# The first norm's sums of squares: six tiles added up on GpSimd, two TensorE matmuls behind the first linear tile in place of eight among the transposes

## The reference

```
def rms_norm(x, g):
    y = x * lax.rsqrt(jnp.mean(x * x, axis=-1, keepdims=True) + EPS)
    return y * g
...
h = rms_norm(x, attn_norm[0])
q, k, v = jnp.split(h @ w_in[0], 3, axis=-1)      # then stick-breaking attention
```

## Time and profile before

| | us |
|---|---|
| median of three runs | 2217.3 (2216.12 to 2218.74) |
| the profiled execution | 2217.15 |
| its span | 2215.4 |
| TensorE busy | 2183.6 (99%) |
| VectorE busy | 1376.4 (62%) |
| ScalarE busy | 794.3 (36%) |
| GpSimd busy | 0.2 |

### The profile page before, as it was taken

One profiled execution on the slowest core, in us unless ns is written; L12 is line 12 of the kernel. 1 busy time (PEld: TensorE's weight loads), 2 busy tenths in 40 slices (PEclk: granted clock), 3 DMA queues, 4 the chain that ended last, 5 costly groups with the idle time before them and its releaser, 6 DMA issues.

```text
span 2215.4 us, 28343 instructions
## 1 busy us (share of the span) xinstructions
PE 2183.6 (99%) x10140; PEld 1728.5 (78%) x10140; DVE 1376.4 (62%) x2081; ACT 794.3 (36%) x1161; POOL 0.2 (0%) x4
## 2 busy tenths in 40 slices
PE   8999999999999999999999999999999999999998
PEld 6777788888886666788888877787788878888887
DVE  6666655554448887755554476687855557888733
ACT  5555432222225555322222224457632223222222
POOL 0000000000000000000000000000000000000000
PEclk9999999999999999999999999999999999999999
DMA  4112133333332222233333332222233332333332
GB/s 143 57 57 57 48 100 99 95 95 92 103 90 58 62 62 58 86 95 97 100 95 97 92 81 67 58 67 67 62 105 95 95 99 87 100 98 95 95 101 91
DMA packets 367107, 188.31 MB, mean 85 GB/s; under 512 B 8968, under 2 KB 366265, under 8 KB 367033
## 3 DMA queue, kind: packets, MB, share of 16 engines
q1 hardware_dynamic: 367033, 187.30, 29.6%
HBM read 185.18 MB, written 2.10 MB: 85 GB/s over the span
## 4 chain that ended last, share of the span: by engine, by line
PE 89%; DVE 6%; ACT 2%; issue 2%; DMA 0%; DVEq 0%; SPq 0%; ACTq 0%
PE lin L1742 78%; PE S L1805 1%; PE ob L1836 1%; PE S L1818 1%; PE S L1915 1%; DVE conv L1381 1%; PE ob L1944 1%; ACT w_hi L534 1%; PE lin L1770 1%; PE misc L1928 1%; PE S L1823 1%; ACT L805 0%; PE S L2071 0%; DVE w_lo L931 0%; PE ob L2099 0%
## 5 line engine op out<-in xcount | busy, mean ns | idle before, releaser
L534 ACT ACTIVATE w_hi<-raw 128x1024 fp32r<-128x1024 f32 x361 | 381.5, 1057 | 844.8 <-PE lin L1742 815.4
L931 DVE TENSOR_TENSOR w_lo<-raw,w_hi 128x1024 fp32r<-128x1024 f32 x361 | 440.9, 1222 | 207.2 <-ACT w_hi L534 206.3
L1742 PE MATMUL lin<-h_hi,w_hi 128*128 128x512 f32 x1928 | 496.1, 399 | 0.6
L1742 PE MATMUL lin<-h_lo,w_hi 128*128 128x512 f32 x1928 | 482.1, 392 | 0.0
L1742 PE MATMUL lin<-h_hi,w_lo 128*128 128x512 f32 x1928 | 477.9, 390 | 0.0
L1742 PEld LDWEIGHTS lin<-h_hi,w_hi 128*128 128x128 f32 x1928 | 358.8, 188 | 89.9 <-issue 15.9
L1742 PEld LDWEIGHTS lin<-h_hi,w_lo 128*128 128x128 f32 x1928 | 361.0, 188 | 74.3
L1742 PEld LDWEIGHTS lin<-h_lo,w_hi 128*128 128x128 f32 x1928 | 358.9, 188 | 74.5 <-issue 1.0
L1742 PE MATMUL lin<-gu_hi,w_hi 128*128 128x512 f32 x528 | 131.4, 389 | 0.0
L1742 PE MATMUL lin<-gu_hi,w_lo 128*128 128x512 f32 x528 | 131.4, 389 | 0.0
L1742 PE MATMUL lin<-gu_lo,w_hi 128*128 128x512 f32 x528 | 131.4, 389 | 0.0
(11 more groups left out here) (380 smaller groups left out, 2172.2 us busy)
## 6 DMA issues: line engine op xcount, KB each, us to landing
raw<-in_w_in_dram SPq DMA_DIRECT2D x108, 512.0 KB, 3.7
raw<-in_w_gate_dram SPq DMA_DIRECT2D x44, 512.0 KB, 3.7
raw<-in_w_up_dram SPq DMA_DIRECT2D x44, 512.0 KB, 3.7
raw<-in_ffn_up_dram SPq DMA_DIRECT2D x44, 512.0 KB, 3.7
raw<-in_w_down_dram SPq DMA_DIRECT2D x32, 512.0 KB, 3.7
raw<-in_w_out_dram SPq DMA_DIRECT2D x24, 512.0 KB, 3.7
raw<-in_ffn_down_dram SPq DMA_DIRECT2D x16, 512.0 KB, 3.7
raw<-in_w_down_dram SPq DMA_DIRECT2D x16, 384.0 KB, 3.4
```

The costliest lines, as they stand in the source:

```text
L534: act.activation(w_hi[u.slot][:, :, :], raw[u.slot][:, :, :], ACT.Copy).then_inc(hi_ready, 1)
L931: dve.tensor_tensor(w_lo[u.slot][:, :, :], raw[u.slot][:, :, :], w_hi[u.slot][:, :, :].bitcast(f32), ALU.subtract).then_inc(lo_ready, 1)
L1742: ins = pe.matmul(acc, (wh, wh, wl)[part][:, k, :], (hi, lo, hi)[part][:, k0 + k, :], start=first and part == 0 and k == 0, stop=last and ...
```

## The change

GpSimd gets six additions. The first adds the squares of tiles 0 and 1 into `xt[0]`, the next five add tiles 2 to 6. Each waits for ScalarE's square (`sq_ready`) and for the addition before it (`x_acc`). Tile 7's square stays in `sq_sum`. TensorE's eight `x_squares` matmuls go; two take their place behind the whole first linear tile, one over `xt[0]` and one over `sq_sum`. ScalarE's square of tile f now waits until GpSimd has read the buffer it overwrites (`x_acc`), and the scale waits for the one `x_sq`.

```
-        x_sq = sem("x_sq")
+        x_sq, x_acc = sem("x_sq"), sem("x_acc")
...
                 if f >= 2:
-                    act.wait_ge(x_sq, f - 1)
+                    act.wait_ge(x_acc, max(f - 2, 1))
...
-            act.wait_ge(x_sq, KT)
+            act.wait_ge(x_sq, 1)
             token_scale(0)
...
+        @block.gpsimd
+        def _(pool):
+            pool.wait_ge(sq_ready, 2 + CREDIT)
+            pool.tensor_tensor(xt[0][:, :], sq[:, :], sq_sum[:, :], ALU.add).then_inc(x_acc, 1)
+            for f in range(2, KT - 1):
+                pool.wait_ge(sq_ready, f + 1 + CREDIT)
+                pool.wait_ge(x_acc, f - 1)
+                pool.tensor_tensor(xt[0][:, :], xt[0][:, :], (sq, sq_sum)[f % 2][:, :], ALU.add).then_inc(x_acc, 1)
...
                 first_rows(range(KT - 2))
-                x_squares(KT - 2)
                 first_rows([KT - 2])
-                x_squares(KT - 1)
                 first_rows([KT - 1])
                 pe.wait_ge(resid, 3 * (R_INIT + 7))
                 linear(At(0), 0, (1, 2), late=late)
+                x_squares()
                 linear(At(0), 1, (0,))
...
-            def x_squares(f):
-                pe.wait_ge(sq_ready, f + 1 + CREDIT)
-                pe.matmul(misc[:, :], table("ones"), (sq, sq_sum)[f % 2][:, :], start=f == 0, stop=f == KT - 1).then_inc(x_sq, 1)
+            def x_squares():
+                pe.wait_ge(x_acc, KT - 2)
+                pe.wait_ge(sq_ready, KT + CREDIT)
+                pe.matmul(misc[:, :], table("ones"), xt[0][:, :], start=True, stop=False)
+                pe.matmul(misc[:, :], table("ones"), sq_sum[:, :], start=False, stop=True).then_inc(x_sq, 1)
...
                 ins.then_inc(x_tr, 1)
-                if f > 1:
-                    x_squares(f - 2)
```

## The result

The changed kernel takes 2222.12 us (median of 18 runs, 2220.19 to 2222.87), the kernel before 2217.15 (18 runs, 2216.02 to 2218.78): ratio 1.0021, 95% interval 1.0014 to 1.0027. It is slower by 5 us. That lies in the range (2216.6 to 2222.4) near its upper end, with five of the 18 runs above it, and beyond the forecast of 2219.6. The profiled execution took 2221.91, its span 2220.1.

A forecast was written before the change was run, and what follows sets the result against it. TensorE was taken as the bound, with the first linear tile's eighth row waiting on weight DMA, ScalarE and VectorE. Net 0.79 (1.72 - 0.93) plus 1.7 for the clock gave 2.5 us on 2217.15: 2219.6, range 2216.6 to 2222.4.

The forecast's parts named there:

- a fall of the clock without turns: Main case: TensorE at 1.2 GHz when the first linear tile starts, GpSimd and VectorE not excluding each other; 2219.6 us, chance 0.38.
- turns and a drop: Rival: `h_lo` and GpSimd's additions exclude each other, and TensorE's clock falls; 2221.0 us, chance 0.24.
- The two squares behind the tile: Two square matmuls behind the first linear tile, where TensorE has no gap, cost 2 x 0.86 = 1.72 us.
- The eighth row's gain: First linear tile's eighth row, freed from the last two square matmuls, ends at 20.98 instead of 21.91: 0.93 us gained.
- What goes ... they return nothing: Six square matmuls before 18.34 return nothing when removed; what follows is bound by weight DMA, ScalarE and VectorE.
- The addition's duration: Each GpSimd addition taken as 1.22 us, bounded by 0.69 and 2.44, from VectorE rows.
- the 1.7 us from which ScalarE's later squares would have waited: Addition length at which GpSimd's fifth sum would be late for ScalarE's square 7 at 19.20, without turns.
- Turns on the port: Rival: VectorE's `h_lo` and GpSimd's additions exclude each other, making `h_hi` 7 1.4 us late; 0.24 with a clock drop.
- The clock: Thin TensorE stretch before the eighth row drops it to 1.2 GHz at the first linear tile, for 3.40 us: 1.7 us.
- The bound of 2.3: Upper bound in us on the cost of TensorE's clock drop at the first linear tile; lower bound 0.
- The late scale, ScalarE's queue: `rsB` by about 28.0, still in time; first softplus 0.3 us later than TensorE's shift, covered by 2.3; cost 0.
- a slow GpSimd: Rival: GpSimd becomes the bound; at 1.8 us an addition with turns, 6.8 us in all, 2223.9; chance 0.11.

The follow-up runs named there:

- e7: Changed kernel plus six idle-time TensorE matmuls, behind the transposes of tiles 6 and 7 and before rows 5 to 7 of the first linear tile; 2220.4 us, ratio 1.0010.
- e8: Changed kernel with six idle-time TensorE matmuls added and GpSimd's additions removed (squares of tiles 0 to 5 left out of the sum); 2218.5 us, ratio 1.0006.
- e4: Kernel before without its first six square matmuls and ScalarE's waits for them, the last two in place, nothing on GpSimd; 2220.0 us, ratio 1.0003.
- e6: Kernel before, reordered only: transposes of tiles 6 and 7 and four first-linear-tile rows issued ahead of tile 4's square; 2217.0 us, ratio 0.9996.
- e2: Changed kernel without GpSimd's additions and ScalarE's waits for them (squares of tiles 0 to 5 left out of the sum); 2221.4 us, ratio 1.0013.
- e9: Changed kernel with GpSimd's six additions reading `xT`, ScalarE's waits removed, squares of tiles 0 to 5 left out of the sum; 2222.5 us, ratio 1.0016.
- e1: Changed kernel plus eleven idle-time TensorE matmuls, behind the transposes of tiles 2 to 7 and before rows 4 to 7; 2220.5 us, ratio 1.0010.
- e11: Changed kernel run again, unedited; 2222.1 us, ratio 1.0017 against the kernel before.

## Why the prediction was right or wrong

The forecast was a fall of the clock without turns (0.38). What happened is the rival "turns and a drop" (0.24), with a dearer clock than either had. The profiled executions give the sum for the 4.13 us at the second linear tile: two square matmuls 1.72, the slow clock 2.77, the eighth row's effective start 0.36 earlier (21.05 + 0.27 against 21.68; e7's 17 matmuls at full clock took 4.15, 0.27 more than 3.88, which is the wait's overhead).

- **The two squares behind the tile: right.** 0.86 each, and all of it on the path.
- **The eighth row's gain: right in itself, overtaken in part.** Predicted 0.93. Without additions (e8) the net with the squares was 0.83 for the predicted 0.79. With them 0.88 is lost, and the weight DMA landed 0.34 earlier in that execution: 0.93 - 0.88 + 0.34 = 0.39, and 0.36 was seen.
- **"What goes ... they return nothing": right beside the other removals.** The eighth row now waits for `h_hi` 7. In the order of before, the six held TensorE's queue: e4 and e6 show 0.5 to 0.6 us to be had there without moving the last two, which is part of the 0.93 and not on top of it.
- **The addition's duration: sized a little low.** 1.22 taken, 1.27 to 1.54 seen, the longer ones held by an `h_lo`. The estimate of 1.35 us from the figures of the Trainium skill (GPSIMD Engine Reference, Elementwise) lies between. The addition stayed under the 1.7 us from which ScalarE's later squares would have waited; only square 2 did, before the weights had landed. (By its own formula the prediction should have put 0.7 and 3.9 us on additions of 1.8 and 2.44 us without turns, not 0.9 and 4.1; nothing here rests on it.)
- **Turns on the port: given 0.24 as a rival, and it happened.** The prediction's own sign for it, `h_lo` late behind additions, is there. Priced at 1.4, it cost 0.88. The prediction began each turn when the last one had ended and gave it its full time; the three handovers that lie on the path overlap by 0.1 to 0.2 us each. The Trainium skill (SBUF — State Buffer, Who interferes with whom) names the pair of instructions, and says that one blocks the other fully for the whole instruction. The trace agrees but for that overlap: full blocking would have held `h_lo` 4 until the addition that began at 15.60 ended at 16.89, and 0.75 more is 17.64; it ended at 17.45, and all 37 end 0.2 us early in this way. The spans on GpSimd are rough, so that part of the 0.2 can lie in the records.
- **The clock: right that it falls, the term mis-sized.** This is the step that failed in size: "Half a clock over 3.40 us costs 1.7." In the trace before, one stretch of 3.4 us was slow between 10.3 us and the last 4. Here 10.24 us were, in both traces of the changed kernel, in e2 and in e9, and 3.3 (e9) to 6.0 (changed kernel) of them lay behind the eighth row's start. In the changed kernel that cost 2.77. The bound of 2.3 was too tight as well. The rows at 23.60 to 27.00, TensorE busy throughout and still at 0.50, show what I had not reckoned with: here the clock was not back while TensorE worked without a gap for 3.4 us.
- **The late scale, ScalarE's queue: right.** The shift at the fifth weight tile (4.18) is that at the second linear tile (4.13) within 0.05.

From there the shift grew to 4.75 at the last linear tile, 0.4 of it between 1570 and 1603 us. Slow-clock stretches elsewhere differ between executions: 1583.8 before, 1556.2 and 1586.9 after, and one near 680 in e1, e2 and e9, across which their shift grows by 1.6 us. Such stretches could make the clusters of the times; no timed run shows where it was slow. Whether the change makes them likelier is open; e11 ended 3.3 behind the kernel before, not 4.75.

The prediction gave 0.84 to a change within 0.2% and 0.14 to a slower kernel; the ratio's interval lies across that bound. The way to more than 4.4 us that I had priced was a slow GpSimd. In fact it took the forecast's two terms, the clock one larger by 1.1, and the rival's 0.88 together, less 0.34 for the weights' earlier landing. That the median is inside the range owes something to luck: its upper end came from turns priced too dear and a clock priced too cheap.

## What to carry to other kernels

Work taken off TensorE while it waits for others can give nothing back, and can cost: what looked like hidden ballast held the clock up here, and 6 us of the dense tile behind the thinned stretch ran at 1.2 GHz. Before matmuls are moved from a stretch that waits to one that does not, count both: their full price where they land, and what the thinner stretch does to the clock at the start of the dense one. An addition handed to GpSimd is not free for VectorE when VectorE's instruction beside it also has two inputs in SBUF; look at whose duration grows, not only at who waits. And look at the timed runs beside the one profile: e4's trace shows a gain, and six of its eleven runs a loss.

## What the runs showed of the hardware

- The granted clock fell to 0.50 for 3.41 us at a time (before, e4) or for 10.24 us (changed kernel, e2, e9, e11). In the last 3.4 us of the changed kernel's slow stretch TensorE had no gap.
- With six idle-time matmuls on constants (448 columns each) it stayed at 1.00 up to 1553 us (e7).
- GpSimd's addition of two 128x512 float32 tiles and VectorE's `h_lo` (two operands in SBUF) take turns: `h_lo` ended 0.55 or 0.56 us after the addition that ran when it started, 37 times in six traces. The addition spans 1.27 to 1.29 us free of it and up to 1.54 held by it; `h_lo` 1.15 to 1.22 and once 1.42, in place of 0.75. VectorE's copies from PSUM kept 0.68 or 0.69.
- The weight DMA's landing moved by up to 1.1 us between executions (13.94 to 15.04) with the same order of issues, more than several of the terms above. It was issued at 9.5 to 10.8 and landed 4.1 to 4.8 us later.
